# A four-layer hybrid diffusion backbone on one core: six rearrangements at stage borders

## The reference, cut to what matters

```python
for i in range(DEPTH):
    m_lat = split(silu(c) @ mod_w[i] + mod_b[i], 6)       # the same for the context with c_ctx
    u = rmsnorm(h, g[0]) * (1 + m[1]) + m[0]
    o = mixer_i(u)                                        # attention, Hyena, windowed attention, attention
    h = h + m[2] * rmsnorm(o, g[1])
    u = rmsnorm(h, g[2]) * (1 + m[4]) + m[3]
    gate, up = split(u @ w_up)                            # 1024 -> 2 x 2816
    f = (silu(dwconv3(gate)) * up) @ w_down
    h = h + m[5] * rmsnorm(f, g[3])
# Hyena's filter: f = sin(z @ w1 + b1); f = sin(f @ w2 + b2); f = sin(f @ w3 + b3); f = f @ w4
```

## Time and profile before

| | value |
|---|---|
| median of three runs | 2201.54 us (2200.75 to 2202.37) |
| the profiled execution's own time | 2201.47 us |
| its span | 2199.7 us |
| TensorE matmul busy | 2129.1 us, 97% of the span |
| VectorE busy | 1448.3 us, 66% |
| ScalarE busy | 885.3 us, 40% |
| chain that ended last | TensorE 82%, VectorE 9%, ScalarE 5%, DMA 3% |
| DMA over the span | 304.44 MB, mean 138 GB/s |

### The profile page before, as it was taken

The page is one execution under the profiler, slowest core; times in us unless marked ns, Lnnn a source line. Parts: engine busy times, 40 slices in busy tenths (PEclk is TensorE's granted clock), DMA queues, the critical chain, the costliest instruction groups (busy, mean ns, idle before and its releaser), DMA issues.

```text
span 2199.7 us, 28738 instructions
## 1 busy us (share of the span) xinstructions
PE 2129.1 (97%) x11692; PEld 1747.4 (79%) x11692; DVE 1448.3 (66%) x2197; ACT 885.3 (40%) x1341; POOL 190.6 (9%) x231
## 2 busy tenths in 40 slices
PE   6999999999999999999999998999999999998998
PEld 4777888888787777988888796588888878968996
DVE  2426557878766675677877656855788775656554
ACT  3337443332244442533332244844333223455543
POOL 0000011111010002011110001101111100100110
PEclk9999999999999999999999999999999999999999
DMA  9560334556542222245546531022555553214554
GB/s 302 181 202 20 115 99 156 167 162 212 200 139 78 87 77 77 77 134 163 170 155 220 173 107 58 21 79 95 162 163 171 193 191 121 97 51 151 178 186 144
DMA packets 224411, 304.44 MB, mean 138 GB/s; under 512 B 6832, under 2 KB 152926, under 8 KB 224152
## 3 DMA queue, kind: packets, MB, share of 16 engines
q1 hardware_dynamic: 219744, 289.77, 40.5%
q0 software_dynamic: 3920, 12.58, 1.7%
q10 hardware_dynamic: 616, 0.26, 0.1%
HBM read 301.47 MB, written 1.11 MB: 138 GB/s over the span
## 4 chain that ended last, share of the span: by engine, by line
PE 82%; DVE 9%; ACT 5%; DMA 3%; issue 2%; ACTq 0%; DVEq 0%
PE lo L655 16%; PE lo L656 15%; PE lo L657 15%; PE lo L753 4%; PE lo L754 4%; PE lo L755 4%; PE hi L753 2%; PE hi L755 2%; PE hi L754 2%; DVE w_lo L1566 2%; ACT w_hi L1202 2%; PE lo L1001 2%; DMA w_raw<-in_ffn_w_down 1%; DMA w_raw<-in_ffn_w_up 1%; PE stat L753 1%
## 5 line engine op out<-in xcount | busy, mean ns | idle before, releaser
L655 PE MATMUL lo<-u_hi,w_hi 128*128 128x512 f32 (+1 forms) x1984 | 703.2, 354 | 8.2 <-DVE w_lo L1566 4.9
L656 PE MATMUL lo<-u_lo,w_hi 128*128 128x512 f32 (+1 forms) x1984 | 691.9, 349 | 0.0
L657 PE MATMUL lo<-u_hi,w_lo 128*128 128x512 f32 (+1 forms) x1984 | 691.5, 349 | 0.0
L1566 DVE TENSOR_TENSOR w_lo<-w_raw,w_hi 128x2048 fp32r<-128x2048 f32 (+1 forms) x182 | 406.6, 2234 | 337.6 <-ACT w_hi L1202 336.2
L1202 ACT ACTIVATE w_hi<-w_raw 128x2048 fp32r<-128x2048 f32 (+1 forms) x182 | 339.8, 1868 | 481.8 <-DMA w_raw<-in_ffn_w_down 259.6
L655 PEld LDWEIGHTS lo<-u_hi,w_hi 128*128 128x128 f32 x1984 | 375.9, 189 | 69.1 <-issue 18.6
L657 PEld LDWEIGHTS lo<-u_hi,w_lo 128*128 128x128 f32 x1984 | 375.9, 189 | 48.2
L656 PEld LDWEIGHTS lo<-u_lo,w_hi 128*128 128x128 f32 x1984 | 376.0, 190 | 47.4 <-issue 1.0
L1583 DVE SCALAR_TENSOR_TENSOR mod_acc<-mod_raw,silu_c,mod_acc 128x512 f32<-128x512 f32 x504 | 394.4, 848 | 7.1 <-DMA mod_raw<-in_mod_w 7.1
L2135 POOL TENSOR_TENSOR mid_lo<-conv,mid_hi 128x512 fp32r<-128x512 f32 (+1 forms) x88 | 117.7, 1358 | 1054.8 <-ACT mid_hi L1545 1054.8
L753 PE MATMUL lo<-w_hi,mid_hi 128*128 128x512 f32 x374 | 147.5, 394 | 3.6 <-DVE u_raw L1657 2.5
(11 more groups left out here) (398 smaller groups left out, 2783.9 us busy)
## 6 DMA issues: line engine op xcount, KB each, us to landing
w_raw<-in_ffn_w_up SPq DMA_DIRECT2D x88, 1024.0 KB, 5.1
mod_raw<-in_mod_w SPq DMA_DIRECT2D x144, 512.0 KB, 3.8
w_raw<-in_ffn_w_down SPq DMA_DIRECT2D x40, 1024.0 KB, 5.1
mod_unit<-in_mod_w SPq DMA_DIRECT2D x24, 1024.0 KB, 6.5
w_raw<-in_a_w_qkv SPq DMA_DIRECT2D x12, 1024.0 KB, 6.8
w_raw<-in_b_w_in SPq DMA_DIRECT2D x12, 1024.0 KB, 5.1
w_raw<-in_a_w_out SPq DMA_DIRECT2D x8, 1024.0 KB, 5.0
w_raw<-in_ffn_w_down SPq DMA_DIRECT2D x8, 512.0 KB, 3.7
```

The lines of the kernel that those rows point to most:

```text
L655: mm(o, h3[:, k, c], x, start=(first and k == 0), stop=False)
L656: mm(o, h3[:, k, c], y, start=False, stop=False)
L657: ins = mm(o, l3[:, k, c], x, start=False, stop=(last and k == nr - 1))
L1566: tt(WL[:, n % 3, 0:words], RAW[:, n % 3, 0:words], WH[:, n % 3, 0:words].bitcast(F32), ALU.subtract).then_inc(lo_ready, 1)
```

## The change

1. The rows of `b_b_in` and `b_conv_b` leave the early blocks (48 rows stay empty and are set to zero by GpSimd) and go to the late ones. The five early transfers left are dealt to two queues: three stay on ScalarE's, two are issued on SyncE's queue ahead of the tokens. Both queues wait for a GpSimd memset first.
2. At the start TensorE runs 8 idle products in place of 12, then 12 between the first turns and unit 0, and 4 ahead of unit 2.
3. In layer 1, stage 0 of the filter moves between the first tiles (after tile 0's second half of columns), and stages 0 to 2 use PSUM bank 5 in place of bank 6.
4. In the last input tile of an attention layer, `exps(i, 0)` moves up to k = 5, in layer 0 ahead of the last `unit_row`.
5. In attention's loop `hi` and `lo` of the second output tile are made in halves, after s = 2 and 3 on ScalarE and after s = 4 and 5 on VectorE.
6. In `x_phase` with four blocks, `u_los` makes six of the eight low parts after block 2 and the last two only after the residual of block 3.

```diff
@@ -41,9 +41,9 @@
 KIND = [i % 3 for i in range(DEPTH)]
 
 
-ROWS = [("norm_g", DEPTH * 4 * KT), ("mod_b", DEPTH * NMOD * KT), ("c", KT), ("c_ctx", KT), ("b_b_in", 3 * KT),
-        ("b_conv_b", 3 * KT), ("ffn_conv_w", DEPTH * 3 * FM), ("ffn_conv_b", DEPTH * FM), ("a_q_gain", 2), ("a_k_gain", 2),
-        ("b_conv_w", 9 * KT), ("c_b_qkv", 10)]
+ROWS = [("norm_g", DEPTH * 4 * KT), ("mod_b", DEPTH * NMOD * KT), ("c", KT), ("c_ctx", KT), (None, 48),
+        ("ffn_conv_w", DEPTH * 3 * FM), ("ffn_conv_b", DEPTH * FM), ("a_q_gain", 2), ("a_k_gain", 2), ("b_b_in", 3 * KT),
+        ("b_conv_w", 9 * KT), ("b_conv_b", 3 * KT), ("c_b_qkv", 10)]
 EARLY = 3
 ROW0 = {}
 _n = 0
@@ -547,6 +547,9 @@
                 sp.dma_start(MG[s][:, :, :], a["mod_w"][0, :, at:at + TW].rearrange(
                     "(k p) n -> p k n", p=P)).then_inc(group_in[s], 16)
 
+            sp.wait_ge(rows_clear, 1)
+            for dst, src in row_loads(a, PR)[0][1::2]:
+                sp.dma_start(dst, src).then_inc(rows_in, 16)
             for t in range(4):
                 src = a["x"] if t < 2 else a["ctx"]
                 sp.dma_start(H[:, t, :], src[0, (t % 2) * P:(t % 2) * P + P, :]).then_inc(x_in if t < 2 else c_in, 16)
@@ -709,6 +712,8 @@
                                  done=(v + 1) * SEQ >= widths[t])
                             if v == 0 and V > 1 and t == 0:
                                 u_turns(sub, 1, range(6))
+                            if v == 1 and t == 0 and sub == 2:
+                                filter_stage(0)
 
             def u_turns(k, v, cs):
 
@@ -840,7 +845,7 @@
 
             pe.wait_ge(rows_in, 16 * N_ROW_DMAS[0])
             turn_rows(range(EARLY))
-            idle_products(12)
+            idle_products(8)
             pe.wait_ge(consts_set, 1)
             pe.wait_ge(par_ready, 1)
             pe.wait_ge(silu_ready, 1)
@@ -883,12 +888,16 @@
                 if p == 3:
                     last.then_inc(tile_done, 1)
 
-            for r in range(2):
-                start_turns(0, r)
-                start_unit(r)
-                unit_cols()
+            start_turns(0, 0)
+            idle_products(12)
+            start_unit(0)
+            unit_cols()
+            start_turns(0, 1)
+            start_unit(1)
+            unit_cols()
+            idle_products(4)
+            start_unit(2)
             idle_products(6)
-            start_unit(2)
             start_part(0, 0)
             unit_cols()
             pe.wait_ge(rows_late, 16 * N_ROW_DMAS[1])
@@ -1046,11 +1055,11 @@
                     if t == 0:
                         pe.wait_ge(tab_in, TAB_AT[1])
                         pe.wait_ge(gr_rows, 2)
-                        mm(bank[6][0:FW, 0:SEQ], FWT[0:FEMB, 0:FW], ZT[0:FEMB, :], start=True, stop=True).then_inc(f_mm, 1)
+                        mm(bank[5][0:FW, 0:SEQ], FWT[0:FEMB, 0:FW], ZT[0:FEMB, :], start=True, stop=True).then_inc(f_mm, 1)
                     else:
                         pe.wait_ge(f_sin, t)
                         w = FW if t == 1 else 2 * FW
-                        mm(bank[6][0:w, 0:SEQ], FWT[0:FW, t * FW:t * FW + w], FA[0:FW, t % 2, :], start=True,
+                        mm(bank[5][0:w, 0:SEQ], FWT[0:FW, t * FW:t * FW + w], FA[0:FW, t % 2, :], start=True,
                            stop=True).then_inc(f_mm, 1)
                 elif t < 5:
                     for x in (2 * t - 6, 2 * t - 5):
@@ -1138,7 +1147,6 @@
                 n0, q0 = FIRST["in", i], PAIR0["in", i]
                 if KIND[i] == 1:
                     first_tiles(n0, q0, 2 * i, (TOK, TOK))
-                    filter_stage(0)
                     filter_stage(1)
                     for t in range(2, 12):
                         tile(n0 + t, q0 + t, TOK, UH, UL, True, True,
@@ -1200,6 +1208,16 @@
                 words = TILES[n][3] * TILES[n][5]
                 act.wait_ge(raw_in[n % 3], 16 * (n // 3 + 1))
                 f(WH[:, n % 3, 0:words], RAW[:, n % 3, 0:words], ACT.Copy).then_inc(hi_ready, 1)
+
+            def hi_half(n, half):
+
+                words = TILES[n][3] * TILES[n][5] // 2
+                part = slice(half * words, (half + 1) * words)
+                if half == 0:
+                    act.wait_ge(raw_in[n % 3], 16 * (n // 3 + 1))
+                ins = f(WH[:, n % 3, part], RAW[:, n % 3, part], ACT.Copy)
+                if half == 1:
+                    ins.then_inc(hi_ready, 1)
 
             def o_square(k, h, b):
 
@@ -1290,7 +1308,8 @@
                 f(MROW[:, r % 2, :], modp[:, TW:2 * TW], ACT.Copy).then_inc(group_rows, 1)
 
             act.dma_start(ident_t[:, :], a["k_ident"]).then_inc(const_in, 16)
-            for dst, src in row_loads(a, PR)[0]:
+            act.wait_ge(rows_clear, 1)
+            for dst, src in row_loads(a, PR)[0][0::2]:
                 act.dma_start(dst, src).then_inc(rows_in, 16)
             act.wait_ge(par_ready, 1)
             act.wait_ge(consts_set, 1)
@@ -1394,12 +1413,13 @@
                                 q_norm(TURNS[i][j])
                         if n0 + t in UNITS and k % 2 == 1:
                             unit_row(UNITS[n0 + t][k // 2])
+                        if t == 5 and k == 5:
+                            exps(i, 0)
                     if KIND[i] == 2 and t == 3:
                         bias_hi(i)
                     if t < 5:
                         hi(n0 + t + 2)
                     else:
-                        exps(i, 0)
                         exps(i, 1)
                     act.wait_ge(tile_done, n0 + t + 1)
                     evac(t)
@@ -1438,8 +1458,8 @@
                         if x == W * s and s >= KN + 2 and (s - KN - 2) % KN == 0:
                             o_hi((s - KN - 2) // KN)
                         evac(x)
-                    if s == 2:
-                        hi(FIRST["out", i] + 1)
+                    if s in (2, 3):
+                        hi_half(FIRST["out", i] + 1, s - 2)
                 for g in range((NH[i] // W - 1 - KN - 2) // KN + 1, GROUPS[i]):
                     o_hi(g)
 
@@ -1566,6 +1586,15 @@
                 tt(WL[:, n % 3, 0:words], RAW[:, n % 3, 0:words], WH[:, n % 3, 0:words].bitcast(F32),
                    ALU.subtract).then_inc(lo_ready, 1)
 
+            def lo_half(n, half):
+
+                words = TILES[n][3] * TILES[n][5] // 2
+                part = slice(half * words, (half + 1) * words)
+                dve.wait_ge(hi_ready, n + 1)
+                ins = tt(WL[:, n % 3, part], RAW[:, n % 3, part], WH[:, n % 3, part].bitcast(F32), ALU.subtract)
+                if half == 1:
+                    ins.then_inc(lo_ready, 1)
+
             def mod(k):
 
                 u, quarter = divmod(k - MOD0, 4)
@@ -1676,7 +1705,7 @@
                 link(nc.vector.reciprocal(R2[:, 1, b:b + 1], R2[:, 0, b:b + 1]))
                 ts(DIAG[:, b, :], ident, R2[:, 1, b:b + 1], None, ALU.mult).then_inc(diag_ready, 1)
 
-            def u_los(k, v):
+            def u_los(k, v, c0=0, c1=KT):
 
                 s, shift, n = slice(v * SEQ, (v + 1) * SEQ), 3 * KT * (k % 2), U0[k] + KT * v
 
@@ -1685,9 +1714,9 @@
                     stt(ULF[:, c, s], u_slot(k, v, c), coef[:, v, k % 2, c:c + 1], UH[:, c, s].bitcast(F32), ALU.mult,
                         ALU.subtract).then_inc(u_diff, 1)
 
-                difference(0)
-                for c in range(KT):
-                    if c + 1 < KT:
+                difference(c0)
+                for c in range(c0, c1):
+                    if c + 1 < c1:
                         difference(c + 1)
                     dve.wait_ge(u_diff, n + c + 1)
                     ts(UL[:, c, s], ULF[:, c, s], modv[:, v, shift + c:shift + c + 1], None, ALU.add).then_inc(u_ready, 1)
@@ -1711,6 +1740,8 @@
                 for b in range(NB):
                     o_gate(k, 1, b)
                     residual(k, b)
+                    if b == 3 and more:
+                        u_los(k + 1, 0, 6, KT)
                     if b == 0:
                         lo(L + 1)
                     if b == 1 and k % 2 and more:
@@ -1718,7 +1749,7 @@
                     if b == NB // 2 and more:
                         if NB == 2:
                             diagonal(k + 1, b)
-                        u_los(k + 1, 0)
+                        u_los(k + 1, 0, 0, KT if NB == 2 else 6)
                     if more and not (b == 1 and NB == 2):
                         diagonal(k + 1, b)
                 lo(L + 2)
@@ -1864,8 +1895,8 @@
                         o_lo((s - KN - 3) // KN)
                     for x in range(W * s, W * s + W):
                         step(x)
-                    if s == 3:
-                        lo(FIRST["out", i] + 1)
+                    if s in (4, 5):
+                        lo_half(FIRST["out", i] + 1, s - 4)
                 for g in range((NH[i] // W - 1 - KN - 3) // KN + 1, GROUPS[i]):
                     o_lo(g)
 
@@ -1903,7 +1934,7 @@
                         dve.wait_ge(f_mm, t + 1)
```

(7 more changed lines are left out.)

## The result

| | before | after |
|---|---|---|
| median, four runs each | 2201.14 us (2199.77 to 2202.37) | 2180.11 us (2177.93 to 2182.26) |
| the profiled execution's own time | 2201.47 us | 2182.26 us |
| its span | 2199.7 us | 2180.5 us |

The ratio is 0.9908 (95% interval 0.9895 to 0.9920). The change is faster by 21.0 us where 15.8 were forecast, and the median lies 0.9 us under the low end of the range, 2181 us. Between the two profiled executions the gain is 19.2 us; that of after was the slowest of its four runs.

A forecast was written before the change was run, and what follows sets the result against it. TensorE, busy 97% of the span, bounds the kernel; only idle or low-clock stretches can go. Start 3.4, filter 3.4, borders 5.7, exponential 0.7 and halves 2.6 sum to 15.8 us: 2201.47 to 2185.7 us, range 2181 to 2191.5 us.

The forecast's parts named there:

- Rows and products: Start: rows land 2.7 us sooner, twelve idle products ahead of unit 0 eat that; gain 0.
- a sign of being wrong, unit 0 later than before: Start: the prediction is wrong if unit 0 runs later than before the change.
- The high clock behind it: Start: `start_turns(0, 1)` and unit 1 halve at the full clock; gain 1.8 us.
- The third term: Start: the 3.4 us slow-clock stretch in the first part of tile 0 goes; gain 1.6 us.
- Filter: Layer 1's filter: VectorE's 1.78 us wait for stage 0 and the slow stretch behind TensorE's wait go; 3.4 us.
- Borders: Six sub-layer borders: TensorE's waits for `w_lo` and the diagonal go; 5.7 us.
- the slower rival: Borders: low part 6 comes late and first tiles stand for it; 2.8 us late undoes everything; chance 0.03.
- Exponential: Last input tile: first exponential done early, VectorE's 0.71 us wait for it goes; 0.7 us.
- Halves: Attention's `hi` and `lo` in halves: 1.6 us in layer 3, 0.8 in layer 0, 0.2 in layer 2; together 2.6 us.
- The rival that they give nothing: Attention: wait for the second `hi` half is as long as the `lo` it replaces; 2188.3 us; chance 0.08.
- The rival that the start gives nothing: Start: rows gain only 0.9 us, low-clock products set unit 0 back; 2189.1 us; chance 0.15.
- the one that the slow stretches stay: Filter and first part: the clock falls all the same, taking 3.2 us from the sum; 2188.9 us; chance 0.10.

The follow-up runs named there:

- one_queue: Changed kernel with all five early row transfers on ScalarE's queue; 2183.39 us.
- seven_dealt: Changed kernel with seven early transfers (384 rows) dealt over the two queues, three ahead of the tokens; 2180.73 us.
- own_half: Changed kernel, but the first half of `lo` waits only for its own half of `hi`; 2182.64 us.
- old_exp: Changed kernel with the first block's exponential behind the last unit's row again; 2181.11 us.
- after_again: The changed kernel measured once more, unedited, as the measure for the others; 2180.04 us.
- old_start: Changed kernel with rows, queues and idle products all as before the change; 2187.31 us.
- old_halves: Changed kernel with `hi` and `lo` of the second output tile made whole again; 2181.94 us.
- old_idle: Changed kernel with idle products as before: twelve behind the rows, six ahead of unit 2, none between first turns and unit 0; 2185.50 us.
- before_plus_4: Kernel before the change with four idle products added between unit 2 and `start_part(0, 0)`; 2199.29 us.
- before_plus_8: Kernel before the change with eight idle products added between unit 2 and `start_part(0, 0)`; 2199.05 us.

## Why the prediction was right and where it failed

**Rows and products: the step that failed.** It is the 0 in "Start: 0 + 1.8 + 1.6", for "what the rows gave, the products eat". The rows came 5.15 us sooner, not 2.7, and above the high end of 4.7, because the dealing counts (one_queue, seven_dealt). The slower turns and the products ate all of that on TensorE, so there the 0 is right. But the term stood for ScalarE's copy of unit 0's row, which I put at 22.5 us out of 21.4 to 24.6. In before ScalarE was late for it by itself, as three lines of before's timeline show that the forecast had not used:

```profile
20.73 1.89 ACT L1202 ACTIVATE w_hi<-w_raw 128x2048 fp32r<-128x2048 f32 x1
...
22.94 0.61 PE L633 MATMUL modp<-ident,mod_rows 128*128 128x2 f32 x4 [2.06 <-ACT mod_rows L1290]
...
32.57 0.47 PE L880 MATMUL lo<-u_hi,w_hi 128*128 128x512 f32 x1 [1.86 <-DVE u_lo L1614]
```

ScalarE went from `hi(0)` straight to the copy, and TensorE waited 2.06 us for it. ScalarE's list hangs on the rows too, and in after `hi(0)` comes 5.1 us sooner:

```profile
15.59 1.89 ACT L1210 ACTIVATE w_hi<-w_raw 128x2048 fp32r<-128x2048 f32 x1
```

So it is now ScalarE that waits, and it copies at 21.13 us. These 1.4 us are what the term of 0 measured; with 1.6 us for the turns and unit 1 and 1.6 us for the first part they make the 4.6 us against 3.4. The copy's move is sure and its size is not: in the four traces with before's start it stands at 21.9 to 22.5 us, in the nine with the changed start (own_half and old_exp among them) at 18.4 to 21.6, as the twelve products took from 2.8 to 4.8 us. The forecast had also named a sign of being wrong, unit 0 later than before. It is met in after (0.2 us later) and not in after_again (1.1 us sooner), and it was a poor sign, since in before unit 0's result lay waiting for ScalarE.

**The high clock behind it** was right for the turns and unit 1, which take 1.14 and 1.07 us in after; that is 1.6 us and not 1.8, as the same two at the high clock in before (1.13 and 1.07 us) could have told. The third term, 1.6 us for the slow stretch in the first part, was met in number, but in part by luck: the stretch was read from one trace, and old_start shows that before's start can run without it.

**Filter:** right, 3.46 us against 3.4, wait and clock both as forecast. The wait left was 0.82 us where I said 1.1 us plus 0.4.

**Borders:** right in place, 6.3 us against 5.7. Low part 6 wasn't late, so the slower rival is refuted; the wait for `w_lo` in the first tiles is 0.2 us at most.

**Exponential:** 0.7 us, as said. The rest of layer 0's attention gained less than worked out: both together 1.1 us of lead against 1.5 (2.1 us in after_again).

**Halves:** layer 3 gave 1.3 us against 1.6, with waits of 0.88 and 0.64 us where I said 1.1 and 0.5. In layer 2 I find no gain. The rival that they give nothing is refuted by old_halves' rows, its time alone would not do it.

**The rest of the miss** is no term of the sum: the forecast put it at nothing. Profile against profile the gain was 3.4 us over the forecast: start +1.2, borders +0.6, layers 0 and 3 and the halves in layer 2 together -0.9, the stretch at layer 2's attention +1.4, and +1.1 in the last layer's MLP, where nothing was edited. Another 1.8 us comes from the medians: that of after lies 2.2 us below its profiled execution, that of before 0.3 us below its own. None of this is firm, since it hangs on the one trace of before. The start is 2.2 us slower in it than in old_start's trace. From 1965 us to the end, where no edit stands, the lead changes by +1.1 us in after and in after_again, by -1.1 in old_idle and +3.6 in old_exp, but also by +1.9 in before_plus_4 and before_plus_8, whose code there is before's: so the +1.1 can't be put down to the change. TensorE's waits for VectorE's `conv` there vary (2.1 us in before, none in old_exp), and I can't say what moves them. Against the later runs of before the same kernel gains 19.9 us (after_again) and not 21.0.

**How much is clock.** Over the 48 executions of before in the four groups the mean granted clock lay between 0.992 and 0.996. The ten at 0.993 took 2200.8 us on average and the eleven at 0.995 took 2198.3, so 1.2 us go with a thousandth. The mean of before is 0.9941, that of the four runs of after 0.9972: at that rate 3.7 us of the 21 are clock. By the price of a stretch (3.4 us at half clock take 0.0008 off the mean and 1.6 us of time, 2.0 us to a thousandth) they are 6.2 us. The forecast's own share was 1.8 + 1.6 + 1.6 = 5.0 us, between the two.

**The range** was too narrow. It took the high end of the start and half of the others', but no account of before's own spread from 2196.4 to 2202.9 us over the four groups, nor of stretches that no edit touches. The rival that the start gives nothing is refuted by old_start's time, the one that the slow stretches stay is refuted for the filter's and stays untested for the first part's.
